# Banded attention in a streaming encoder step: division moved to the output rows, low parts moved to VectorE, VectorE's queue reordered

## The reference

```
q = rmsnorm(q.reshape(bsz, t, 8, 64), q_norm);  k = rmsnorm(k..., k_norm)
s = einsum(qc, kb) * 64 ** -0.5 + bias          # own chunk and 8 chunks before it
p = softmax(where(valid, s, NEG), axis=-1)
o = einsum(p, vb)
y = concat([rmsnorm(y_a), rmsnorm(o), rmsnorm(y_c)]) @ w_out
```

## Time and profile before

| | us |
|---|---|
| Median of 3 runs (1675.35 to 1684.78) | 1679.13 |
| Profiled execution | 1680.23 |
| Its span | 1678.5 |
| TensorE busy in the span | 1585.2 |
| VectorE busy | 1012.9 |
| ScalarE busy | 653.5 |
| GpSimd busy | 305.2 |

### The profile page before, as it was taken

The page is one execution under the profiler, slowest core; times in us unless marked ns, Lnnn a source line. Parts: engine busy times, 40 slices in busy tenths (PEclk is TensorE's granted clock), DMA queues, the critical chain, the costliest instruction groups (busy, mean ns, idle before and its releaser), DMA issues.

```text
span 1678.5 us, 27557 instructions
## 1 busy us (share of the span) xinstructions
PE 1585.2 (94%) x11172; PEld 1545.9 (92%) x11172; DVE 1012.9 (60%) x1481; ACT 653.5 (39%) x1146; POOL 305.2 (18%) x354
## 2 busy tenths in 40 slices
PE   6999999997888899999779999999999999999999
PEld 6999999995777799998669999999999999999999
DVE  6625876536888754225653477666666658656653
ACT  5521021126787632214552253333333433333332
POOL 1011000002221010000430004444444421010110
PEclk8999999987999999999999999999999999999999
DMA  7424111002110043201042214433334586454563
GB/s 241 143 89 159 50 39 38 26 1 92 36 37 33 26 138 138 89 26 51 1 148 100 90 55 152 147 143 141 142 142 166 202 281 235 123 165 147 155 211 114
DMA packets 63667, 189.36 MB, mean 113 GB/s; under 512 B 7873, under 2 KB 13049, under 8 KB 63409
## 3 DMA queue, kind: packets, MB, share of 16 engines
q1 hardware_dynamic: 37904, 91.11, 17.1%
q0 software_dynamic: 25648, 96.65, 16.0%
HBM read 138.58 MB, written 54.12 MB: 115 GB/s over the span
## 4 chain that ended last, share of the span: by engine, by line
PE 81%; DVE 7%; ACT 5%; DMA 4%; issue 3%; POOL 1%; SPq 0%; ACTq 0%; DVEq 0%; POOLq 0%
PE ps L452 33%; PE ps L2605 19%; PE ps L2626 17%; PE ps L2163 3%; PE ps L481 2%; DMA a<-wdn 2%; PE ps L2504 2%; PE ps L2356 1%; ACT scores L1168 1%; PE ps L2334 1%; DVE pt_lo L1759 1%; PE ps L2472 1%; PE ps L503 1%; PE ps L2318 1%; DVE scores L1738 1%
## 5 line engine op out<-in xcount | busy, mean ns | idle before, releaser
L452 PE MATMUL ps<-A_hi,w_hi 128*128 128x364 f32 x768 | 174.0, 335 | 0.0
L452 PE MATMUL ps<-A_lo,w_hi 128*128 128x364 f32 x768 | 171.1, 331 | 0.0
L452 PE MATMUL ps<-A_hi,w_lo 128*128 128x364 f32 x768 | 170.7, 331 | 0.0
L393 DVE TENSOR_TENSOR w_lo<-w_raw,w_hi 128x1024 fp32r<-128x1024 f32 x43 | 52.5, 1223 | 150.0 <-ACT w_hi L389 149.6
L389 ACT ACTIVATE w_hi<-w_raw 128x1024 fp32r<-128x1024 f32 x42 | 44.3, 1057 | 241.7 <-PE ps L452 136.2
L452 PEld LDWEIGHTS ps<-A_lo,w_hi 128*128 128x128 f32 x768 | 135.1, 190 | 0.0
L452 PEld LDWEIGHTS ps<-A_hi,w_lo 128*128 128x128 f32 x768 | 135.0, 190 | 0.0
L452 PEld LDWEIGHTS ps<-A_hi,w_hi 128*128 128x128 f32 x768 | 134.2, 191 | 0.0
L2605 PE MATMUL ps<-t_hi,wq_hi 128*128 128x272 f32 x480 | 99.9, 290 | 2.3 <-DVE hid_stage L2059 2.3
L2605 PE MATMUL ps<-t_lo,wq_hi 128*128 128x272 f32 x480 | 99.9, 290 | 0.0
L2605 PE MATMUL ps<-t_hi,wq_lo 128*128 128x272 f32 x480 | 99.7, 289 | 0.0
(11 more groups left out here) (342 smaller groups left out, 4087.6 us busy)
## 6 DMA issues: line engine op xcount, KB each, us to landing
w_raw<-slabs SPq DMA_DIRECT2D x68, 512.0 KB, 4.0
quads_d<-quad_sum POOLq DMA_DIRECT2D x64, 272.0 KB, 2.9
w_raw<-wdn POOLq DMA_DIRECT2D x32, 512.0 KB, 4.0
r_raw_a<-quads_d SPq DMA_DIRECT2D x56, 272.0 KB, 3.1
r_raw_b<-quads_d SPq DMA_DIRECT2D x56, 272.0 KB, 3.0
quads_d<-hid_stage POOLq DMA_DIRECT2D x48, 272.0 KB, 2.9
Y<-xT POOLq DMA_DIRECT2D x16, 546.0 KB, 4.6
y_d<-Y POOLq DMA_DIRECT2D x16, 546.0 KB, 3.2
```

The costliest lines, as they stand in the source:

```text
L393: e.tensor_tensor(WL[:, par], RAW[:, par], WH[:, par].bitcast(F32), ALU.subtract).then_inc(s.w_lo, 1)
L452: ins = e.matmul(PS[:, 3 * par + c, 0:CH], wt[:, wpar, w], xt[:, col:col + CH], start=(first and n == 0 and m == 0), stop=(last and n == l ...
```

## The change

The softmax's division is made once for each group on the output rows in place of on each unit's scores. `exps` writes its row sums into a buffer of a whole group, `exp_recip` inverts them in two parts (units 0 to 5, units 6 to 8), ScalarE lays the inverses out (`rec_heads`), and TensorE transposes them as three further items of each group (x = 9, 10 in turn 7, x = 11 in turn 0 of the next group, or after the last unit). VectorE multiplies them into Y (`o_divide`). `cache_lo` and `qk_lo` of groups 1 to 3 go from GpSimd's queue to VectorE's. VectorE's turn n is now `pt_lo(n)`, `biased(n+2)`, low parts, items of n. `ya_norm` moves from units 27 and 28 to units 29 and 30.

```diff
 # GpSimd
-                if j:
-                    g.wait_ge(s.bias_ready, 2 * j + 2)
-                    cache_lo(g, j)
-                    g.wait_ge(s.kc_lo, 2 * j + 2)
-                    g.wait_ge(s.qk2_lo, 2 * j)
-                    qk_lo(g, j, 0)
                 g.wait_ge(s.k_nrm, 3 * j + 3)
                 g.dma_start(o_k[j], QKV[4 + j][:, 512:TOK]).then_inc(s.kv_out, 16)
-                if j:
-                    qk_lo(g, j, 1)
 # order of the items
+        def items(n):
+            j, i = divmod(n, 9)
+            done = [(j - 1, 11)] if i == 0 and j else []
+            new = [(j + 1, x) for x in CHUNKS.get(i, ())] if j < 3 else []
+            return done + new + ([(j, 9), (j, 10)] if i == 7 else [])
+        def item_bank(x):
+            return 6 if x % 3 == 1 else 7
+        YA_UNIT = (29, 30)
 # ScalarE
+            def rec_heads(j, part):
+                b0, b1 = (0, 6) if part == 0 else (6, 9)
+                e.wait_ge(s.bc_done, N_ACT_BC + (ITEM[j + 1, 5] if j < 3 else ITEM[2, 11]))
+                e.wait_ge(s.rec_done, 2 * j + part + 1)
+                e.activation(RX[:, b0:b1], EREC[:, 9 * j + b0:9 * j + b1].unsqueeze(3).to_broadcast([P, b1 - b0, 2, 64]),
+                             ACT.Copy).then_inc(s.rx_ready, 1)
...
+                if i == 6 and j:
+                    rec_heads(j - 1, 0)
+                if i == 8:
+                    rec_heads(j - 1, 1)
...
-                    if n >= 2:
-                        e.wait_ge(s.rec_done, n - 1)
 # VectorE
-            def normalise(n):
...
+            def exp_recip(j, b0, b1):
+                e.wait_ge(s.exp_done, 2 * (9 * j + b1))
+                e.reciprocal(EREC[:, 9 * j + b0:9 * j + b1].rearrange("p b h -> p (b h)"),
+                             ESUM[:, 9 * j + b0:9 * j + b1].rearrange("p b h -> p (b h)")).then_inc(s.rec_done, 1)
+            def o_divide(j, c):
+                lo, hi, blocks = BC[c]
+                hi = min(hi, TOK)
+                e.wait_ge(s.o_used, 2 * (9 * j + blocks[-1] + 1))
+                e.wait_ge(s.bc_done, cnt.bc + 1)
+                e.tensor_tensor(y(2 + j)[:, lo:hi], y(2 + j)[:, lo:hi], PS[:, 6 if c == 1 else 7, 0:hi - lo],
+                                ALU.mult).then_inc(s.o_div, 1)
...
             biased(0)
-            normalise(0)
+            biased(1)
             for n in range(N_U):
-                if n + 1 < N_U:
-                    biased(n + 1)
+                if n % 9 == 6:
+                    exp_recip(n // 9, 0, 6)
+                if n % 9 == 8:
+                    exp_recip(n // 9, 6, 9)
                 pt_lo(n)
-                if n + 1 < N_U:
-                    normalise(n + 1)
+                if n + 2 < N_U:
+                    biased(n + 2)
                 if n == 1:
                     cache_lo(e, 0)
+                if n < 27 and n % 9 == 3:
+                    cache_lo(e, n // 9 + 1)
+                if n < 27 and n % 9 in (4, 6):
+                    qk_lo(e, n // 9 + 1, (n % 9 - 4) // 2)
+                for j, x in items(n):
+                    item(j, x)
 # TensorE
                 transposes(n)                      # waits for the exponentials, not for the division
+                if n - 1 in YA_UNIT:
                     e.wait_ge(s.bc_used, cnt.used(cnt.bc))
                 if n:
+                    consumed(*last[7])
                     values(n - 1)
                 if n + 2 < N_U:
                     scores(n + 2)
+                for j, x in items(n):
...
             values(N_U - 1)
+            e.wait_ge(s.o_used, 2 * N_U)
+            item(3, 11)
```

More of the change, by code:

```diff
@@ L1712, in v_lo, with item @@
                                     ALU.subtract).then_inc(s.v_lo, 1)
[L1714 to L1726, removed]
+            def item(j, x):
+                assert cnt.bc - N_DVE_BC + 1 == ITEM[j, x]
+                if x < 3:
+                    heads_nrm(QKV[j], GQ[:, 0:1], s.q_nrm, x)
+                elif x < 6:
+                    heads_nrm(QKV[4 + j], par_col("k_norm"), s.k_nrm, x - 3)
+                elif x < 9:
+                    v_lo(j, x - 6)
+                else:
+                    o_divide(j, x - 9)
+                cnt.bc += 1
+            N_DVE_BC = cnt.bc
             def biased(n):
@@ L2274, in _, with consumed @@
                     n_rc += 1
-            def prepare(j, x):
+            def consumed(j, x):
                 which, c = divmod(x, 3)
-                used(cnt.bc - (0, 2, 1)[c])
-                if j == 0 and x == 1:
-                    e.wait_ge(s.stat_read, cnt.stat)
[L2282 to L2289, removed]
+                if which < 2:
+                    e.wait_ge((s.q_nrm, s.k_nrm)[which], 3 * j + c + 1)
+                elif which == 2:
+                    e.wait_ge(s.v_lo, 4 * j + c + (2 if c == 2 else 1))
+                else:
+                    e.wait_ge(s.o_div, 3 * j + c + 1)
@@ L2290, in prepare, with item @@
+            def item(j, x):
+                which, c = divmod(x, 3)
+                bank = item_bank(x)
+                if last[bank]:
+                    consumed(*last[bank])
+                elif bank == 7:
+                    e.wait_ge(s.bc_used, cnt.bc)
+                else:
+                    e.wait_ge(s.bc_used, cnt.bc - 2)
+                    e.wait_ge(s.stat_read, cnt.stat)
+                if which == 2:
                     for b in range(3 * c, 3 * c + 3):
                         w = P if b < 8 else 64
-                        ins = e.transpose(PS[0:w, 6 if c == 1 else 7, (b % 3) * P:(b % 3 + 1) * P],
+                        ins = e.transpose(PS[0:w, bank, (b % 3) * P:(b % 3 + 1) * P],
@@ L2294, in prepare @@
                 ins.then_inc(s.bc_done, 1)
                 cnt.bc += 1
+                last[bank] = (j, x)
+            last = {6: None, 7: None}
             def scores(n):
@@ L2358, in values @@
                 ins.then_inc(s.pv_done, 1)
[L2360 to L2375, removed]
             for x in range(9):
-                prepare(0, x)
+                item(0, x)
             e.wait_ge(s.tile_read, S_OUT)
```

91 lines of the change are left out of this document (51 added, 40 removed).

## The result

The change makes the kernel slower: 1693.17 us median (13 runs, 1687.36 to 1705.53) against 1680.82 for the kernel before in the same series. The ratio is 1.0086, with a 95% interval of 1.0066 to 1.0107; it is estimated from the fast runs, without one of 3047 us of the kernel before, and is not the quotient of the medians, 1.0073. 1692 was forecast. The profiled execution took 1690.95 us.

The account below looks back on a forecast made before the run. No engine was saturated over the stage; a ring of queues waiting for each other bound it. Group 0 +3.4, groups 1 and 2 4.85 each, last group -0.5 made +12.6 on 1680.2, written as 1692 at the median; range 1676 to 1703.

Parts of the forecast that it names:

- The ring: Attention: item, `values`, `scores`, `biased`, low part, next item wait in a circle; groups 1 and 2 each cost 4.85 us more.
- The sum: Whole attention: 3.4 + 2 x 4.85 - 0.5 = +12.6 us on the profiled execution's 1680.2, giving 1692.8.
- The last group: From `values(26)` to `out_part`: 44.7 us against 45.16, -0.5; two turns set by VectorE at 5.35 fall to 4.9 and 4.3.
- The prices: Work added: `o_divide` 0.55 us each, `rec_heads` together 5.4, `qk_lo` 1.28, `cache_lo` 0.69; VectorE in all 18.4 less.
- The end: End of attention: TensorE stands about 2.4 us until ScalarE, with two copies ahead, writes the last rows, then does item 11.
- Rival two, VectorE's load: Attention: 18.4 us less VectorE load shows as time, 1661 us, or 1670 with half of it; chance 0.13.
- Rival three, only the low parts: Only the low parts in front of items cost, the rest is hidden: +3 us, so 1682; chance 0.22.
- Rival four, the clock: Stalls of 1.7 us twice a group bring a granted clock of 0.89: +12 us over three groups, 1704; chance 0.10.
- The rule on the shared port: GpSimd and VectorE lock each other out; moving work to VectorE gives time back; counted 0, else 0.4 us lower (group 0).

Follow-up runs that it names:

- low_last: The changed kernel with VectorE's low parts of turns 3, 4 and 6 behind the items of their turn; ratio 1.0025 to the kernel before.
- before_cache: The kernel before with only `cache_lo` of group 0 moved to the start of turn 1, ahead of `biased(2)`; ratio 0.9977, median 1676.25 us.
- before_low: The kernel before with only the low parts of groups 1 to 3 moved to VectorE, in turns 3, 4 and 6; ratio 1.0037.
- double_low: The changed kernel with an unread reduction of the same width behind each `qk_lo` of groups 1 to 3; ratio 1.0163 to the kernel before.
- low_pool: The changed kernel with the low parts of groups 1 to 3 back on GpSimd; ratio 1.0015 to the kernel before.
- items_first: The changed kernel with the items ahead of `biased(n+2)`, behind `pt_lo(n)`, and the low parts last; ratio 1.0043 to the kernel before.
- old_order: The changed kernel with VectorE's turn as `biased(n+1)`, `pt_lo(n)`, items, low parts; ratio 1.0099 to the kernel before.
- mix: The changed kernel with items ahead of `biased` in turns 0, 1, 2, 4, 6, low parts last, ScalarE's last rows between its two copies; ratio 1.0059.
- mix_pool: As mix, but with the low parts of groups 1 to 3 back on GpSimd; ratio 1.0018 to the kernel before.
- best: As mix, but turn 6's item behind `biased` again and `cache_lo` of group 0 at the start of turn 1; ratio 1.0026, median 1685.85 us.
- best_pool: As best, but with the low parts of groups 1 to 3 on GpSimd; ratio 0.9996 to the kernel before, median 1680.14 us.

## Why the prediction was right

- *The ring.* It holds in the places forecast. Start of `values` to start of `values`, by turn, in us:

| turn | 0 | 1 | 2 | 3 | 4 | 5 | 6 | 7 | 8 | group |
|---|---|---|---|---|---|---|---|---|---|---|
| before, group 2 | 3.03 | 4.93 | 3.90 | 6.29 | 4.80 | 6.02 | 4.92 | 4.79 | 2.68 | 41.36 |
| forecast | 4.55 | 3.85 | 4.5 | 6.7 | 6.3 | 6.1 | 6.6 | 4.9 | 2.7 | 46.2 |
| after, group 1 | 4.37 | 3.74 | 4.35 | 6.74 | 6.27 | 6.09 | 6.52 | 4.56 | 2.72 | 45.36 |
| after, group 2 | 4.33 | 4.80 | 4.94 | 6.75 | 6.27 | 7.63 | 6.53 | 4.61 | 2.71 | 48.57 |
| low_last, group 1 | 4.38 | 3.73 | 4.35 | 6.09 | 5.07 | 6.13 | 5.31 | 4.56 | 2.71 | 42.33 |

  Turns 3, 4, 6 and 8 are within 0.1 us of the forecast in both groups, turn 5 in group 1. Turn 7 was taken 0.3 too long: its two items began at 2.65 (480.89 in group 1), when Y was written, but were read by 4.24 and not at 4.65. Turns 1 and 2 fit in group 1 and are 0.95 and 0.4 over the forecast in group 2; there the granted clock was at the level of 1.2 GHz from 492.5 to 495.9, as it was in turn 5 from 513.0 to 516.4. The waits show the ring in sum, from 385 to 585 us (total, times, longest):

```profile
DVE scores L1769 <- issue: 30.9, 23, 3.4
...
PE ps L2415 <- DVE k_raw L1731: 5.5, 3, 1.8
PE ps L2415 <- DVE v_lo L1742: 5.4, 3, 1.8
```

  In low_last the last two are 1.9 and 1.8 us, with the longest 0.7 and 0.6.
- *The sum.* Group 0 to `values(8)` +2.65 (3.4 forecast), groups 1 and 2 together +10.2 (9.7), the last group 44.84 us, -0.3 (-0.5). Together +12.5 against +12.6. That this fits to 0.1 us is luck. These are groups 1 or 2 in which the clock was full, by run, in us:

| before | before_cache | before_low | after | double_low | low_last | low_pool | items_first | old_order | mix | mix_pool | best | best_pool |
|---|---|---|---|---|---|---|---|---|---|---|---|---|
| 41.36 | 41.33 | 42.82 | 45.36 | 47.83 | 42.33 | 42.40 | 42.6 | 44.54 | 42.9 | 41.5 | 42.24 | 41.91 |

  So the ring costs +4.0 a group, against 4.85 forecast: turn 7 and a few tenths in turns 0 to 2. The rest came from the clock. Stretches at the lower level cost the trace after 3.2 us in group 2 (48.57 against 45.36) and 1.3 in turn 8 of the last group (3.91 against 2.63 to 2.67 in low_last and best). They cost the trace before 1.0 in group 1 and 0.5 in turn 4 of group 0 (5.34 against 4.79 in before_cache). Without these the +12.5 would be some +9.6, an estimate: the forecast had the mechanism about 3 us too dear and the clock, which it put at nothing, made it up.
- *The last group* is a second cancellation. Its turns 4, 5 and 6, which VectorE had set at 5.35 us, fell to 3.80, 4.18 and 4.16, by 3.9 us; the forecast gave them 1.5. Turn 7 rose from 5.07 to 6.48, turn 8 by 1.3 with the clock. And the end was over-priced, see below.
- *The prices.* `o_divide` 0.528 each (0.55 taken), `rec_heads` 5.5 us (5.4), `qk_lo` 1.29 with 1.21 to the next start, `cache_lo` 0.69 and 0.60 paced: as taken. VectorE fell by 16.9 and not by 18.4. The records of neighbours overlap, and busy time counts an overlap once: left out of the trace before, the multiplies and reciprocals take 34.5 us of busy time with them and not 37.1, and the added work brings 16.3 and not 18.7. That makes 18.2, so two errors of the sum cancel; the last 1.3 us were not traced.
- *The end.* TensorE waits for ScalarE's last rows and then does item 11, as walked, but it stands 0.87 us and not 2.4. From `values(35)` to `out_part` it is 3.35 us, against 2.15 before:

```profile
578.11 0.46 ACT L1209 ACTIVATE Y<-ps 64x64 f32<-64x64 f32 x2
```

```profile
578.62 0.55 PE L2350 MATMUL ps<-ident,rstd_heads 128*128 128x128 f32 x3 [0.87 <-ACT Y L1209]
```

  Reordering ScalarE's tail brings 0.3 us: this distance is 3.04 in best. The last group of best is 1.2 us shorter than that of the change (43.68 against 44.84) mainly because turn 8 ran at the full clock.
- *Rival two, VectorE's load*, falls: 16.9 us less of it, and the span is longer; low_pool and low_last differ by 0.001 though the first has 9.7 us less on VectorE (985.4 against 995.1). *Rival three, only the low parts*: they are the larger share, 3.0 of the 4.0 us of a group (low_last), but 1.0 us remains in each, where it expected the shorter path from the exponentials to pay for everything else. It named the right first cause and had no price for the ring through `biased`. *Rival four, the clock*: no group ran whole at a lower clock, but stretches of it made about 3 of the 12.5 us in this pair of traces; it held in part, see below.
- *The rule on the shared port* (the Trainium skill, SBUF — State Buffer, "SBUF: two separate sides") would have moving GpSimd's work to VectorE give time back. No run shows such a return: before_low against before and mix against mix_pool show a cost (1.0037 to 1, and 42.9 to 41.5 us a group), low_last against low_pool no difference (1.0025 to 1.0015). The one VectorE record that the trace before shows stretched beside GpSimd's low parts is the first of the two multiplies that the prediction named, 0.93 us where its like takes 0.55; with the division moved, that instruction is gone, and in low_pool nothing is stretched.

What stays open: no kernel has the division without its three further items a group, so that it "buys nothing" is shown of the whole (best_pool 0.9996 against before_cache 0.9977, with 41.9 and 41.3 us in group 1), and not what its items and its saved latency are worth each. Nor is it known how the two would compare at one granted clock: the means were 0.972 and 0.976. Nor was it tried whether two buffers for the scores, or a third bank for items, would open the ring.

## What to carry to other kernels

In a ring of in-order queues an instruction costs by whose wait it stands in front of, more than by its duration: find for each consumer what is queued ahead of it and when that can start. Put what frees a shared bank ahead of work that nobody awaits at once; that gave 3 us a group here. It is no rule for everything else: to put it ahead of `biased` as well gave nothing (items_first), and work that stands last still cost 1.4 us a group (mix against mix_pool). An engine's saved 17 us are worth nothing if it spends them waiting ahead of something that was ready. And a sum that meets the measured total may do so by two errors, so compare it term by term. Look, too, at what a low-ranking instruction releases: the best edit of this study moves one `cache_lo` ahead of `biased` so that a load starts earlier, and adds no work at all.

## What the runs showed of the hardware that I had not expected

TensorE's granted clock fell from the level of 2.4 GHz to that of 1.2 for a few microseconds at a time, in places that differ from kernel to kernel. In the stage before it did so from 418.5, 459.4 and 534.5 us, in the stage after from 492.5, 513.0 and 571.0, beside a longer stretch at the start of both, which ended at 404.8 and 403.8. First one of before, then the three of after:

```profile
459.40:462.80 3.40, 3.40 (x18) 3.40 (x18) 2.77 (x7) 1.75 (x3) 2.52 (x1) 0.50 0.00 0
```

```profile
492.50:495.90 3.40, 3.40 (x18) 3.40 (x17) 2.19 (x6) 1.29 (x3) 0.00 (x0) 0.50 0.00 0
513.00:516.40 3.40, 3.40 (x18) 3.08 (x19) 1.08 (x3) 0.60 (x4) 0.44 (x1) 0.50 0.22 87
571.00:574.40 3.40, 3.40 (x19) 3.17 (x18) 3.03 (x6) 1.44 (x3) 0.00 (x0) 0.51 0.02 5
```

TensorE was busy for the whole of these four. Such a stretch cost 0.5 us (turn 4 of group 0 before) to 1.65 us (turns 1 and 2 of group 2 after, 4.80 and 4.94 in place of 3.74 and 4.35). Each of the six began within 2.3 us after TensorE had gone on from a wait: of 3.51, 1.72 and 1.52 us before, and of 0.97, 1.83 and 2.48 us after. But the stage has 17 waits over 0.9 us before and 19 after, and most were followed by no such stretch; what decides is open.

The runs' mean granted clocks say more than one profile. They were 0.974 for the kernel before in all three series of experiments, 0.967 to 0.973 for every kernel with the division or with VectorE's low parts (the change itself 0.972), and 0.976 for before_cache. Among the runs of one kernel, 0.001 less goes with mostly 1 to 1.5 us more (the slope through them). By this estimate 2 to 3 of the 14 us between the means of the change and of the kernel before go with the clock, nearly all of best's 1.0026, and about 2 of the 4 us by which before_cache is faster. That the edits lowered the clock by their waits is likely, but not shown. A group should be compared with one in which the clock was full.
